# Forty prompt tokens instead of thirty-two by gathered value rows in a decoder layer's PEER stage

## The chip, the cores and the metric

The kernel runs on one core of a Trainium2 chip. The metric is the device time of one execution, in microseconds; lower is better. Three timed executions of the kernel before are given by their median. One further execution was taken with the hardware profiler; all rows of the trace are from that one.

## The reference, cut to what matters

One decoder layer is computed for 256 prompt tokens and 32 sample tokens (8 sequences of 4), D = 1024. After attention, convolution and projections comes PEER, a mixer with 16,384 experts. Each token picks 16 experts in each of 8 heads, so 128 per token.

```python
def chunk(xc):
    ...
    eid = jnp.take_along_axis(cand_id, top_j, axis=-1)
    gate = jax.nn.softmax(top_s, axis=-1)
    act = jax.nn.gelu(jnp.einsum('chkd,cd->chk', u_emb[eid], xc).astype(F32))
    return jnp.einsum('chk,chkd->cd', (gate * act).astype(v_emb.dtype), v_emb[eid])
```

`u_emb` and `v_emb` have 16,384 rows of 1024 numbers. Everything is float32.

## The kernel before

**Experts as tiles.** The 16,384 experts are 128 tiles of 128 experts; "expert c" below means tile c, 128x1024 numbers, 512 KB. The kernel does not gather `u_emb`: it computes every token's product with every expert. The *score stage* (from about 420 us) does this for tile 0 to 127: for all T = 288 tokens, a matmul with the stationary tile and the tokens as moving columns. To keep float32 accuracy in a faster matmul type, a tile is cut into a high and a low half; high x high, high x low and low x high are added, 24 matmuls of 288 columns per tile (lines 2300, 2301, 2307). The *output stage* (from about 864 us) does the weighted sum with the tiles of `v_emb`: for the TW = 224 prompt tokens that are done densely, the weights (gate x score, zero where a token did not pick the expert) are the moving columns. A tile costs eight matmuls `high` of 2 x 224 columns (value high with weights high and low, line 2358) and eight `lower` of 224 columns (line 2361).

**Tokens by gathered rows.** TG = 64 tokens, the 32 samples and the last 32 prompt tokens, don't pass through the output matmuls. Each has only 128 picks. 32 tokens x 128 picks are spread over the 128 partitions in 4 groups of 32 tokens, so 32 columns of picks for each set. For each column j POOL gathers a row of `v_emb` into each partition (`gather_row`, line 797, 512 KB) and the score of that pick from a copy in DRAM (`gather_score`, line 802, 4 bytes per partition). VectorE multiplies four columns of scores with their gates (`scale_picks`, line 1831) and adds row times weight to a sum (`add_row`, line 1840). At the end a matmul with the small matrix `fold` (four identities below one another) adds the partitions of each token: for the prompt set in `prompt_rows` (line 2396) between output experts 125 and 126, for the samples in `samples` (line 2388). The picks of the prompt set are computed in partitions 96 to 127 and brought into the pick tables by four moves, SBUF to SBUF, that SP issues after the stores of expert 31 (line 647, semaphore `moved`).

**Gates.** The dense weights need a gate matrix of 128 experts x 128 tiles per token. It is built beside score experts 32 to 87, in MIXED = 56 units of four tokens, one per expert: VectorE makes one-hots (lines 1768, 1769), TensorE multiplies them (`gate_tokens`, line 2336, two halves per unit, behind the high and the low matmuls of the expert), ScalarE copies (line 1158), VectorE adds (line 1778).

**Scores.** ScalarE applies gelu (line 1151) and SP stores the scores of experts 0 to 87 in DRAM (lines 637, 639; afterwards only the part of the 64 tokens, line 667), because the gates aren't ready. These 88 are read back in 22 reloads of four (`load_again`, line 661), into NACT = 5 buffers, three of which lie in the row buffers 2 to 4; VectorE multiplies them into the gates (`weights`, line 1805). Scores 88 to 127 are multiplied as they come (line 1810). Before the change reload j is issued at score expert 91 + 2j, the last three behind the tile loads of output experts 0 to 2. Products 72 to 87 are done beside output experts 0 to 15.

**What sets the order.** Each engine has a program written out by hand, with semaphores between them. Tiles come through a ring of R = 4 slots: `load_expert(c)` on SP (line 628) waits until both halves of tile c are cut, then loads tile c+4 into its slot. Then SP waits for the gelu of c and issues its stores, so whatever stands ahead of `load_expert` on SP delays tile and stores. ScalarE cuts the high halves (line 1090), at most two tiles ahead of TensorE, as `split` has two buffers; the gelu of expert c waits for the stores of expert c-2. The low halves are cut by POOL in the score stage (`cut_low`, line 784) and by VectorE in the output stage (`value_low`, line 1824). In the output stage ScalarE also makes the high weights (line 1192) and VectorE the low ones (`low`, line 1819); `high` waits for `w_lo`, `lower` for `lo_ready`. VectorE's order per output expert is `low`, `value_low`, for experts 0 to 15 one `weights`, and at the experts in ADD_AT an `add_row`, every fourth with `scale_picks` before it:

```python
FIRST_ADD, LAST_ADD = 6, NSUB - 5
ADD_AT = [FIRST_ADD + j * (LAST_ADD - FIRST_ADD) // (TG - 1) for j in range(TG)]
```

POOL's order after its last cut is: zero the sums, rows 0 and 1, wait for all score stores, scores 0 to 3, rows 2 to 4 (each as soon as its reload buffer is free), then for each further four columns: wait for `scale_picks` of the four before, four scores, four rows (each when the row five before it is added).

## Time and profile before

| what | value |
|---|---|
| timed executions | 1203.85 us median of 3 (1203.81 to 1205.47) |
| the profiled execution, its own time | 1208.57 us |
| its span, first to last instruction | 1206.8 us |
| TensorE busy | 1167.5 us |
| VectorE busy | 994.2 us |
| POOL busy | 709.6 us |
| ScalarE busy | 587.2 us |
| bytes moved by DMA | 278.73 MB, mean 231 GB/s |

TensorE is PE, VectorE DVE, ScalarE ACT, GpSimd POOL, SyncE SP; SPq is SP's queue of DMA issues. Busy time is the time in which an engine executes something; a matmul's record is longer than the step to the next one, since they overlap, so the pitch (start to start) is what counts. A releaser in brackets is what ended an idle time. The mean granted clock of a stretch is given as a share of 2.4 GHz, 1.00 being full.

### The profile page before, as it was taken

Reading aid. Unit: us, or ns where it says so; the run is one execution under the profiler, and the core shown is the slowest. Engines: PE = TensorE matmul, PEld = TensorE weight load, DVE = VectorE, ACT = ScalarE, POOL = GpSimd, SP = SyncE. Lnnn points to the kernel's source line nnn. Section 1 sums busy time; section 2 is a strip of 40 time slices with the busy share of each in tenths; the row PEclk is TensorE's granted clock in tenths of the full one; section 3 lists DMA queues with packets and bytes.
Section 4 is the critical chain, followed back from the end, with each engine's and each line's share of the span. In section 5 each row is a group of like instructions: output and inputs, shape, how many; then the busy total and the mean of one; then the engine's idle time right before and its main releaser. Section 6 shows DMA issues by size and latency. Waiting matters only on the chain. (4 is left out here: it accounts for less than half of the span.)

```text
span 1206.8 us, 27394 instructions
## 1 busy us (share of the span) xinstructions
PE 1167.5 (97%) x8823; PEld 1107.9 (92%) x8823; DVE 994.2 (82%) x2194; ACT 587.2 (49%) x1005; POOL 709.6 (59%) x377
## 2 busy tenths in 40 slices
PE   4999999989999999999999999999989999999998
PEld 3898888989989999999999999999989999999997
DVE  4899977866755999969999994998888888878886
ACT  2342445666444344445555554444455555555553
POOL 0475565612755667766666667777766556656531
PEclk9999999999999999999999999999999999999999
DMA  9796685424744356665555556777888899989883
GB/s 358 255 301 220 204 269 194 144 75 141 258 150 140 129 191 208 211 192 189 179 182 178 182 186 199 239 240 256 280 287 315 321 348 326 328 304 328 305 306 121
DMA packets 116800, 278.73 MB, mean 231 GB/s; under 512 B 33216, under 2 KB 54944, under 8 KB 116352
## 3 DMA queue, kind: packets, MB, share of 16 engines
q1 hardware_dynamic: 102928, 237.74, 58.6%
q0 software_dynamic: 12080, 36.51, 8.4%
q10 hardware_dynamic: 1728, 3.68, 0.9%
q8 instruction: 34, 0.56, 0.2%
q14 instruction: 30, 0.25, 0.1%
HBM read 259.41 MB, written 18.42 MB: 230 GB/s over the span
## 5 line engine op out<-in xcount | busy, mean ns | idle before, releaser
L784 POOL TENSOR_TENSOR split<-ring,split 128x1024 fp32r<-128x1024 f32 x128 | 310.2, 2423 | 132.0 <-ACT split L1090 132.0
L1090 ACT ACTIVATE split<-ring 128x1024 fp32r<-128x1024 f32 x256 | 271.6, 1061 | 147.9 <-PE ps L2358 72.1
L717 POOL TENSOR_TENSOR split<-ring,split 128x1024 fp32r<-128x1024 f32 x77 | 188.4, 2450 | 208.0 <-ACT split L901 207.9
L2300 PE MATMUL ps<-h2r,split 128*128 128x288 f32 x1024 | 278.5, 297 | 0.7 <-ACT big L1116 0.5
L2301 PE MATMUL ps<-h2r,split 128*128 128x288 f32 x1024 | 278.7, 296 | 0.0
L2358 PE MATMUL ps<-h2r,split 128*128 128x448 f32 x1016 | 230.9, 369 | 4.3 <-DVE h2r L1819 4.1
L2358 PEld LDWEIGHTS ps<-h2r,split 128*128 128x128 f32 x1016 | 182.3, 189 | 17.7 <-DVE h2r L1819 5.7
L2300 PEld LDWEIGHTS ps<-h2r,split 128*128 128x128 f32 x1024 | 193.0, 188 | 1.2 <-ACT big L1116 0.8
L2301 PEld LDWEIGHTS ps<-h2r,split 128*128 128x128 f32 x1024 | 192.5, 188 | 0.0
L1151 ACT ACTIVATE act<-ps 128x288 f32<-128x288 f32 x124 | 51.1, 412 | 218.3 <-PE ps L2307 218.2
L2307 PE MATMUL ps<-h2r,split 128*128 128x288 f32 x1024 | 156.6, 295 | 0.0
L1824 DVE TENSOR_TENSOR split<-ring,split 128x1024 fp32r<-128x1024 f32 x128 | 155.9, 1218 | 0.0
L2307 PEld LDWEIGHTS ps<-h2r,split 128*128 128x128 f32 x1024 | 141.6, 188 | 0.3 <-POOL split L784 0.3
L2361 PEld LDWEIGHTS ps<-h2r,split 128*128 128x128 f32 x1016 | 134.2, 192 | 3.3
L797 POOL DMA_INDIRECT big<-in_stream,pick_at x64 | 92.7, 1449 | 72.1 <-DVE big L1840 52.0
L2361 PE MATMUL ps<-h2r,split 128*128 128x224 f32 x1016 | 134.7, 274 | 0.0
L901 ACT ACTIVATE split<-ring 128x1024 fp32r<-128x1024 f32 x85 | 89.7, 1055 | 63.0 <-DMA ring<-in_stream 52.8
L802 POOL DMA_INDIRECT pick_act<-s_act_dram,pick_at x64 | 93.1, 1455 | 43.1 <-DVE pick_act L1831 20.7
L1769 DVE SCALAR_TENSOR_TENSOR hot<-ps,parts 128x256 fp32r<-128x256 f32 x224 | 107.1, 478 | 0.0
L1328 DVE SCALAR_TENSOR_TENSOR ps<-big,ps 128x256 f32<-128x256 f32 x232 | 95.7, 487 | 1.0
L1962 PE MATMUL ps<-h2r,split 128*128 128x288 f32 x552 | 90.9, 305 | 2.2 <-ACT split L901 1.2
L1819 DVE TENSOR_TENSOR h2r<-big,h2r 128x224 fp32r<-128x224 f32 x127 | 49.6, 391 | 47.6 <-ACT h2r L1192 35.8
(308 smaller groups left out, 1769.6 us busy)
## 6 DMA issues: line engine op xcount, KB each, us to landing
ring<-in_stream SPq DMA_DIRECT2D x371, 512.0 KB
big<-in_stream SPq DMA_DIRECT2D x20, 512.0 KB, 7.8
act_dram<-act SPq DMA_DIRECT2D x88, 112.0 KB, 1.7
big<-act_dram SPq DMA_DIRECT2D x17, 448.0 KB, 3.9
s_act_dram<-act SPq DMA_DIRECT2D x128, 32.0 KB, 1.5
parts<-act_dram SPq DMA_DIRECT2D x5, 448.0 KB
big<-in_cache_k SPq DMA_DIRECT2D x16, 128.0 KB, 2.5
big<-in_cache_v SPq DMA_DIRECT2D x16, 128.0 KB, 3.4
```

The source lines that it names most:

```text
L717: nc.gpsimd.tensor_tensor(split[:, n % 2, 1], ring[:, POS[CUT[n]] % R, :], split[:, n % 2, 0].bitcast(f32), ALU.subtract).then_inc(lin_lo, 1)
L784: nc.gpsimd.tensor_tensor(split[:, (n + ODD) % 2, 1], ring[:, slot_of(n), :], split[:, (n + ODD) % 2, 0].bitcast(f32), ALU.subtract).then_ ...
L802: pool.indirect_dma_start(pick_act[:, j:j + 1], None, s_act_dram, bass.IndirectOffsetOnAxis(ap=pick_at[:, 1, j:j + 1], axis=0))\
L1090: nc.scalar.activation(split[:, (n + ODD) % 2, 0], ring[:, slot_of(n), :], ACT.Copy).then_inc(hi_ready, 1)
L1328: ins = V.scalar_tensor_tensor(acc if j < CW - 1 else y[:, k, 0:TP], zp[:, k, j:j + TP], w, acc, ALU.mult, ALU.add)
L1769: return V.scalar_tensor_tensor(hot1[:, slot], iota_ps.unsqueeze(1).to_broadcast([P, 2, P]), parts[:, 0, col], parts[:, 2:4, col].to_broad ...
L1824: V.tensor_tensor(split[:, (n + ODD) % 2, 1], ring[:, slot_of(n), :], split[:, (n + ODD) % 2, 0].bitcast(f32), ALU.subtract).then_inc(lo_r ...
L2300: MM(out, u_hi[:, k], h_hi[:, k], start=(k == 0), stop=False)
L2301: last = MM(out, u_hi[:, k], h_lo[:, k], start=False, stop=False)
L2307: last = MM(out, u_lo[:, k], h_hi[:, k], start=False, stop=(k == KC - 1))
L2358: return MM(out, v[0][:, k], w, start=first, stop=last)
L2361: return MM(ps[k][:, 0:TW], v[1][:, k], w[:, 0], start=False, stop=False)
```

## The change

TC = 8 further prompt tokens go by gathered rows, so TG is 72 and TW 216. The eight lie with their 128 picks in 16 groups of 8 partitions, which makes 8 more columns (64 to 71), with tables, a third sum and a fold matrix of their own. MIXED is 54; experts 86 and 87 have no gate unit, 88 scores are still stored. SP issues 16 further moves. The 22 reloads are all issued in the score stage, at experts 89 to 93 and then every second one. POOL's first two row gathers stand before its cuts of experts 124 and 125. The memset of the sums is VectorE's. VectorE does `low` and `value_low` of output expert 0 before the product of score 127. The adds begin at output expert 8.

```diff
...
-TG = 2 * TS
+TC = 8
+TG = 2 * TS + TC
 TW = T - TG
 TURN = BEFORE - R
-AFTER = NSUB - MIXED - BEFORE
-assert BEFORE % R == 0 and MIXED % R == 0 and AFTER % R == 0 and NSUB % R == 0
-
-
-EARLY = (BEFORE + MIXED) // R
-NSTORED = BEFORE + MIXED
+NSTORED = BEFORE + -(-MIXED // R) * R
+AFTER = NSUB - NSTORED
+assert BEFORE % R == 0 and MIXED % 2 == 0 and AFTER % R == 0 and NSUB % R == 0
+
+
+EARLY = NSTORED // R
 LEFT_OVER = R
 AGAIN = (NSTORED // R - LEFT_OVER) * R
-assert NSTORED // R - LEFT_OVER + 1 <= 2 * (AFTER // R) - 1
+AGAIN_AT = [1, 2, 3, 4] + list(range(5, AFTER, 2))
+assert len(AGAIN_AT) >= NSTORED // R
...
             for part in range(4):
-                sp.dma_start(pick_at[part * TS:(part + 1) * TS, :, TS:TG], aside_u[P - TS:P, :, part * TS:(part + 1) * TS])\
+                sp.dma_start(pick_at[part * TS:(part + 1) * TS, :, TS:2 * TS],
+                             aside_u[P - TS:P, :, part * TS:(part + 1) * TS]).then_inc(moved, 16)
+            for part in range(P // TC):
+                sp.dma_start(pick_at2[part * TC:(part + 1) * TC], aside_u[P - TS - TC:P - TS, :, part * TC:(part + 1) * TC])\
                     .then_inc(moved, 16)
...
                     sp.wait_ge(gate_copied, 2 * MIXED)
-                    sp.wait_ge(moved, 16 * 5)
+                    sp.wait_ge(moved, 16 * (5 + P // TC))
                 else:
...
                     sp.dma_start(s_act_rows[g * R + n], act[:, n % 2, TW:T]).then_inc(act_stored[n % 2], 16)
-                    again = (g - EARLY) * 2 + n // 2 - 1
-                    if n % 2 and 0 <= again <= NSTORED // R - LEFT_OVER:
-                        load_again(again)
+                    if (g - EARLY) * R + n in AGAIN_AT[:NSTORED // R]:
+                        load_again(AGAIN_AT.index((g - EARLY) * R + n))
                 load_expert(NSUB + n, n)
-                if n < LEFT_OVER - 1:
-                    load_again(NSTORED // R - LEFT_OVER + 1 + n)
...
                 pool.indirect_dma_start(rows[:, j % NROW], None, value_rows,
-                                        bass.IndirectOffsetOnAxis(ap=pick_at[:, 0, j:j + 1], axis=0))\
+                                        bass.IndirectOffsetOnAxis(ap=mine_of(pick_at, pick_at2, slice(j, j + 1))[:, 0], axis=0))\
                     .then_inc(row_in[j % NROW], 16)
             def gather_score(j):
-                pool.indirect_dma_start(pick_act[:, j:j + 1], None, s_act_dram,
-                                        bass.IndirectOffsetOnAxis(ap=pick_at[:, 1, j:j + 1], axis=0))\
+                pool.indirect_dma_start(mine_of(pick_act, pick_act2, slice(j, j + 1)), None, s_act_dram,
+                                        bass.IndirectOffsetOnAxis(ap=mine_of(pick_at, pick_at2, slice(j, j + 1))[:, 1], axis=0))\
                     .then_inc(score_in, 16)
-            pool.wait_ge(gate_copied, 2 * MIXED)
-            nc.gpsimd.memset(s_sum, 0.0).then_inc(zeroed, 1)
-            pool.wait_ge(moved, 16 * 5)
-            for j in range(NROW - NACT + 2):
-                gather_row(j)
+            pool.wait_ge(moved, 16 * (5 + P // TC))
+            for n in range(R):
+                if n < NROW - NACT + 2:
+                    gather_row(n)
+                cut_low(NSUB - R + n, n, u_done, NSUB - R + (n - 1))
             for s in range(2):
...
             with eng.Fori(BEFORE // R, (BEFORE + MIXED) // R) as g:
-                turn(g, True)
+                turn(g, R)
+            if MIXED % R:
+                turn((BEFORE + MIXED) // R, MIXED % R)
             turn(NSTORED // R, False, stored=False, first=True)
...
             settle()
-            step(V.tensor_scalar(s_expert[:, 1], s_expert[:, 1], float(TS), None, ALU.add))
+            step(V.tensor_scalar(s_expert[:, 1], s_expert[:, 1], float(TS + TC), None, ALU.add))
+            for at, col in ((P - 2 * TS, TC - TS), (P - TS, TC)):
+                mine = theirs[at - part.start:at - part.start + TS, 1]
+                step(V.tensor_scalar(mine, mine, float(col), None, ALU.add))
+            step(V.tensor_reduce(fold2, ident[:, :].rearrange("p (g t) -> p t g", t=TC), AX.X, ALU.add))
             step(V.tensor_scalar(theirs[:, 0], theirs[:, 0], float((NLIN + NSUB) * P), None, ALU.add))
...
...
+            step(V.memset(s_sum, 0.0))
             done = 0
             for c in range(NSTORED, NSUB):
+                if c == NSUB - 1:
+                    low(0, 0, True)
+                    dve.wait_ge(lo_ready, NSUB)
+                    value_low(0, 0, u_done, NSUB - 1)
                 dve.wait_ge(gelued, c + 1)
                     done += 1
...
+            settle()
                 cols = slice(part * R, (part + 1) * R)
+                mine = mine_of(pick_act, pick_act2, cols)
                 dve.wait_ge(score_in, 16 * R * (part + 1))
-                V.tensor_tensor(pick_act[:, cols], pick_act[:, cols], pick_gate[:, cols], ALU.mult).then_inc(s_weighted, 1)
+                V.tensor_tensor(mine, mine, mine_of(pick_at, pick_at2, cols)[:, 2].bitcast(f32), ALU.mult).then_inc(s_weighted, 1)
...
                     dve.wait_ge(row_summed, j)
-                V.scalar_tensor_tensor(total, rows[:, slot], pick_act[:, j:j + 1], total, ALU.mult, ALU.add)\
+                V.scalar_tensor_tensor(total, rows[:, slot], mine_of(pick_act, pick_act2, slice(j, j + 1)), total, ALU.mult, ALU.add)\
                     .then_inc(row_summed, 1)
-            FIRST_ADD, LAST_ADD = 6, NSUB - 5
+            FIRST_ADD, LAST_ADD = 8, NSUB - 5
             ADD_AT = [FIRST_ADD + j * (LAST_ADD - FIRST_ADD) // (TG - 1) for j in range(TG)]
-            dve.wait_ge(zeroed, 8)
             j = 0
                     c = g * (2 * R) + i
-                    low(c, i % R, c == 0)
-                    value_low(c, i % R, *((u_done, NSUB) if c < 2 else (o_done, c - 1)))
+                    if c:
+                        low(c, i % R)
+                        value_low(c, i % R, *((u_done, NSUB) if c < 2 else (o_done, c - 1)))
                     if c < R * LEFT_OVER:
...
                     scores(g * R + (BEFORE + n), n, gates=lambda pair: gate_tokens(g * R + n, n, pair))
-            with pe.Fori((BEFORE + MIXED) // R, NSUB // R) as g:
+            for n in range(R if MIXED % R else 0):
+                mixed_at = MIXED // R * R + n
+                scores(BEFORE + mixed_at, n,
+                       gates=(lambda pair: gate_tokens(mixed_at, n, pair)) if mixed_at < MIXED else None)
+            with pe.Fori(NSTORED // R, NSUB // R) as g:
                 for n in range(R):
...
                 for k in range(KC):
-                    MM(ps[k][:, TW:TP], s_sum[:, 1, k * P:(k + 1) * P], fold[:, :], start=False, stop=False)
+                    MM(ps[k][:, TW:TW + TC], s_sum[:, 2, k * P:(k + 1) * P], fold2, start=False, stop=False)
+                    MM(ps[k][:, TW + TC:TP], s_sum[:, 1, k * P:(k + 1) * P], fold[:, :], start=False, stop=False)
             for n in range(R):

...
```

The functions `low` and `value_low` are unchanged and stand further up, so that the loop over the direct products can call them. `mine_of` picks the table of columns 0 to 63 or that of columns 64 to 71.

## Rows read from the trace of the kernel before

**Rows 1.** The page's part 1: busy us, share of the span, instructions.
```profile
PE 1167.5 (97%) x8823; PEld 1107.9 (92%) x8823; DVE 994.2 (82%) x2194; ACT 587.2 (49%) x1005; POOL 709.6 (59%) x377
```

**Rows 2.** The chain in order of time, output stage: start us, us, what.
```profile
1023.81 1.63 PE ps L2358 x8
1026.32 1.63 PE ps L2358 x8
```

**Rows 3.** TensorE's timeline, experts 34 and 35 with a gate unit: start us, us, line.
```profile
537.94 1.22 PE L2307 MATMUL ps<-h2r,split 128*128 128x288 f32 x8
541.63 1.22 PE L2307 MATMUL ps<-h2r,split 128*128 128x288 f32 x8
```

**Rows 4.** Stretches of the output stage: busy us (instructions) by engine, granted clock, DMA share, GB/s.
```profile
970.00:1010.00 40.00, 40.00 (x257) 38.15 (x256) 34.56 (x44) 22.03 (x32) 22.56 (x18) 1.00 0.97 347
1090.00:1130.00 40.00, 40.00 (x257) 38.10 (x256) 34.50 (x45) 21.91 (x32) 25.48 (x18) 1.00 0.89 310
```

**Rows 5.** The chain, fold of the prompt's gathered rows, 16 matmuls of 32 columns.
```profile
1192.08 1.71 PE ps L2396 x16
```

**Rows 6.** SP's timeline; lines 647 and 595, ns min/median/max; landing for line 661.
```profile
530.08 2.71 SPq L647 DMA_DIRECT2D pick_at<-big  x4
533.20 0.36 SPq L628 DMA_DIRECT2D ring<-in_stream  x1
...
L647 SPq DMA_DIRECT2D pick_at<-big x4: 598/606/767, 530.1 to 532.2; - x4
L595 SPq DMA_DIRECT2D big<-in_cache_v x16: 372/381/935, 46.8 to 175.9; - x16
...
DMA to landing us min/median/max: 3.7/3.9/4.2
```

**Rows 7.** Timelines of TensorE and VectorE in the gate stage; in brackets the idle time before.
```profile
542.68 0.40 PE L2336 MATMUL ps<-hot 128*128 128x256 f32 x2
...
530.81 0.35 DVE L1768 TENSOR_SCALAR hot<-ps,parts 128x128 fp32r<-128x128 f32 x1 [7.90 <-PE ps L2336]
```

**Rows 8.** TensorE's timeline at the junction of the stages, and the stretch around it.
```profile
858.36 1.23 PE L2307 MATMUL ps<-h2r,split 128*128 128x288 f32 x8
...
861.56 1.23 PE L2307 MATMUL ps<-h2r,split 128*128 128x288 f32 x8
864.71 2.73 PE L2358 MATMUL ps<-hot,split 128*128 128x448 f32 x8 [1.93 <-DVE hot L1819]
...
868.89 1.78 PE L2358 MATMUL ps<-h2r,split 128*128 128x448 f32 x8
...
862.00:869.00 7.00, 5.08 (x23) 4.60 (x23) 3.52 (x9) 2.69 (x4) 3.18 (x5) 0.76 0.90 325
```

**Rows 9.** Timelines of TensorE, VectorE and POOL around the stop at 902 us.
```profile
899.32 0.99 PE L2358 MATMUL ps<-h2r,split 128*128 128x448 f32 x4
...
905.15 2.34 PE L2358 MATMUL ps<-h2r,split 128*128 128x448 f32 x8 [3.15 <-DVE h2r L1819]
...
908.96 2.20 PE L2358 MATMUL ps<-h2r,split 128*128 128x448 f32 x8
...
903.25 0.16 DVE L1831 TENSOR_TENSOR pick_act<-pick_act,pick_at 128x4 f32<-128x4 f32 x1 [3.85 <-DMA pick_act<-s_act_dram,pick_at]
...
885.35 5.22 POOL L797 DMA_INDIRECT big<-in_stream,pick_at  x1 [8.05 <-DVE big L1805]
```

**Rows 10.** VectorE's instructions per output expert, page's part 5 and line 1840.
```profile
L1824 DVE TENSOR_TENSOR split<-ring,split 128x1024 fp32r<-128x1024 f32 x128 | 155.9, 1218 | 0.0
L1819 DVE TENSOR_TENSOR h2r<-big,h2r 128x224 fp32r<-128x224 f32 x127 | 49.6, 391 | 47.6 <-ACT h2r L1192 35.8
L1840 DVE SCALAR_TENSOR_TENSOR big<-big,pick_act x64: 1274/1280/1328, 882.1 to 1184.0; 128x1024 f32<-128x1024 f32 x64
```

**Rows 11.** POOL's cut and row gather, page's part 5.
```profile
L784 POOL TENSOR_TENSOR split<-ring,split 128x1024 fp32r<-128x1024 f32 x128 | 310.2, 2423 | 132.0 <-ACT split L1090 132.0
L797 POOL DMA_INDIRECT big<-in_stream,pick_at x64 | 92.7, 1449 | 72.1 <-DVE big L1840 52.0
```

More of the change, by code:

```diff
@@ L376, in build, with mine_of @@
         NROW = 5
+        s_sum = tail.take(3, D)
         rows = tail.take(NROW, D)
-        s_sum = tail.take(2, D)
         act_odd = tail.take(R, TW)
+        pick_at2 = tail.take(3, TC, dt=u32)
+        pick_act2 = tail.take(TC)
+        fold2 = tail.take(TC)
+        def mine_of(tile, tile2, cols):
+            return tile[..., cols] if cols.start < 2 * TS else tile2[..., cols.start - 2 * TS:cols.stop - 2 * TS]
         aside = rows[:, NROW - 1, 0:3 * P].rearrange("p (w n) -> p w n", n=P)
```

26 lines of the change are left out of this document (13 added, 13 removed).

## The prediction, made before the changed kernel was built or run

> **What bounds the kernel now.** I read the busy times, then the chain and timeline of TensorE, then the stretches, then the queues around each place that the diff touches. TensorE is busy for 97% of the span [rows 1], so time is won or lost only where it executes less or stands still. Busy isn't peak, so look at its pitch. In the output stage an expert is eight 448-column and eight 224-column matmuls; the first eight take 1.63 us and the whole repeats every 2.51 us [rows 2]. In the score stage an expert takes 3.20 us, with a gate unit in it 3.69 us [rows 3, 8]. Both stages run at TensorE's pitch, except where a queue is late. Two such places stand out: the junction of the stages [rows 8] and a stop at 902 us [rows 9]. The DMA queues (310 to 347 GB/s in the output stage, share 0.89 to 0.97) and VectorE (34.5 of 40 us) come next [rows 4].
>
> **The change, part by part** (minus is time saved).
>
> 1. *Narrower matmuls.* Each high matmul has 16 columns less, each low one 8. The widths give the price of a column: 1.63/8 = 203.75 ns at 448, (2.51-1.63)/8 = 110 ns at 224, so 0.42 ns per column, the full 2.4 GHz [rows 2]. An expert saves 8 x 24 x 0.4167 = 80 ns, 128 of them 10.2 us. The low matmul would go from 110 to 107 ns. The nearest row for a floor is the fold: 16 matmuls of 32 columns in 1.71 us, 107 ns each [rows 5]; it is just reached. If something near that floor holds the low one at 110 already, only the high ones gain: 6.8 us. I take **-10.2**, other end -6.8.
> The Trainium skill (TensorE: Matmul & The Clock Gate, LDWEIGHTS) puts a weight load at its columns over 1.2 GHz, 107 ns for 128. The fold's row agrees. By that rule the whole 10.2 us comes, and one column less on the low side would bring nothing.
>
> 2. *Two gate units fewer* (54 for 56): 3.69-3.20 = 0.49 us each [rows 3, 8]. **-1.0**.
>
> 3. *The junction.* The last eight score matmuls begin at 861.56, the first output matmul at 864.71, after 1.93 us of idling for VectorE's low weights; the first expert then takes 4.18 us instead of 2.51, at a mean granted clock of 0.76 between 862 and 869, so part of it ran at 1.2 GHz [rows 8]. The change does low(0) and value_low(0) ahead of the last direct product, which they don't need. Their inputs, ScalarE's high halves, are made during the last two score experts. Gone: 1.93 + 1.67 = **-3.6**; ends 0 and -3.6. Next late are the low weights of expert 1, behind the last product and two reload products: some 2 us after gelu, and expert 0 lasts 2.4.
>
> 4. *The stop at 902.* VectorE waited 3.85 us for the second four score gathers, TensorE then 3.15 us, and it restarted slowly: 5.83 and 3.81 us for two experts against 5.03, 4.6 us lost [rows 9]. POOL had come late to those gathers: it held the fifth row gather for VectorE's products of reload 19 and then needed 5.22 us for it, where 1.45 is the mean [rows 9, 11]. Now all reloads are issued within the score stage, the first adds move from expert 6 to 8 and the fifth from 13 to 14, and POOL's fifth row gather falls before the first add: about 3.5 us of slack more against 3.85 missing. Against that, experts 8 to 15 carry five adds beside the reload products: VectorE's work is 8 x (0.39+1.22+0.39) + 5 x 1.28 = 22 us by durations [rows 10], some 20 with the overlap of neighbours, in 19.5 us, and POOL finds few gaps. I take **-3.5**; ends -4.6 and 0.
>
> 5. *Fold of the eight tokens*: eight more calls, 16 matmuls of few columns: **+1.7** [rows 5].
>
> 6. *Sixteen more moves on SP.* SP finished the stores of expert 31, issued four moves from 530.08 (2.71 us, 0.68 each), and only then the tile load of expert 32's slot, at 533.20 [rows 6]. Now 20 moves stand there. A move of 8 partitions isn't in the trace. The nearest row is the four that are there, over 32 partitions: 0.60 us at least, 0.77 at most, and 0.05 between two; a copy over all 128 partitions on this queue takes 0.38 [rows 6]. I take 0.65, by the nearest: 16 x 0.65 = 10.4 us, so the load goes out at 543.6. It brings expert 36's tile. A 448 KB reload lands after 3.9 us [rows 6], 512 KB so after some 4.4; then ScalarE's cut, 1.1, and 0.1 for the signal: 549.2. TensorE was ready for expert 36 behind the gate matmuls of 542.68, at 542.95 [rows 7]. Behind the moves stand also expert 32's stores, for which the gelu of 34 waits, then its gate copies, VectorE's sum and one-hots, and TensorE's gates in expert 35; they too come to 549. So 6.2 us idle. The restarts after 1.9 and 3.15 us of idling cost 1.67 and 1.3 us [rows 8, 9]: 1.7 more. **+7.9**. Ends: at 0.42 each the moves take 6.7, 2.5 us idle, 4.2 in all; at 0.82 (0.77 and 0.05) 13.1, 9.0 idle, 10.7 in all. Nothing or a gain is excluded: the gelu of 34 can't pass the stores behind the moves.
>
> 7. *VectorE's picks* get two column shifts and one reduction, before the gates, where VectorE then stood idle for 7.90 us [rows 7]: hidden, **0**; without that cover 1 us. The memset leaves POOL for VectorE, where the wait for expert 88's gelu hides it. POOL's first two gathers go between its last four cuts: a cut takes 2.42 of 3.20 us, a gather 1.45 with 0.3 around it, so POOL is late by 0.5 to 1 us twice, about what its product was early. **+0.3**, ends 0 and 2. The reloads start two experts earlier, the first five in a row: 442 + 524 KB in 3.2 us is 302 GB/s, under the 347 that the queues carried [rows 4]: 0.
>
> 8. *More to carry in less time.* Each output expert brings a 524 KB tile, and a row gather now falls on each 1.62 experts (115 over 71) instead of each 1.86. That is 848 KB in 2.435 us, 348 GB/s, where it was 807 KB in 2.51 us, 321. One stretch ran at 347 with TensorE never idle, at a share of 0.97 [rows 4]: the load fits with almost nothing over. From 868.89 to the fold at 1192.08 are 323.2 us for 125 experts, 314.2 at their pitch: beside the stop, 4.4 us went in small delays [rows 5, 8]. VectorE's work per expert goes from 0.39+1.22+0.54 x 1.28 = 2.30 of 2.51 us to 2.40 of 2.435 by durations [rows 10], in truth some 0.2 us less in both. I put **+3.5**, nearly the 4.4 once more; ends 0 and 15.
> POOL's long gathers are those that meet VectorE without a gap [rows 9]. The Trainium skill (SBUF — State Buffer, Terms) has the two arbitrate for a port pair that is held for a whole instruction, the loser blocking. The trace agrees in that a gather that took 5.22 us ended during an add.
>
> Sum: -10.2-1.0-3.6-3.5+1.7+7.9+0.3+3.5 = **-4.9 us**. The profiled execution took 1208.57 us (span 1206.8 and 1.8 around it) and would take 1203.7. The three timed runs have a median of 1203.85, 4.7 lower; I take that difference over: **1199.0**.
>
> **Rivals.**
> - *Cheap moves.* At 0.42 us a move, term 6 is 4.2: 1195.3. For: a move has 768 bytes, a sixteenth of the four. Against: the four have little either and took longer than a 128 KB copy [rows 6]. Chance 0.2.
> - *The low matmuls don't shrink*, so the change doesn't do what it says: +3.4, 1202.4. For: 110 is near 107 ns. Against: 17 ns stand over the pure columns in both widths. Chance 0.1.
> - *The stop returns*, POOL starving behind a VectorE that has no gap in experts 8 to 15: term 4 is 0, and 1.5 us go at the third group: 1204.0. For: 22 us by durations in 19.5. Chance 0.1.
> - *The DMA queues become the bound, slower than before.* At 330 GB/s 848 KB take 2.57 us, 115 experts 295.5 us against 280.0: +15.5 in place of 3.5, 1211.0. It decides below 348 GB/s, eats the whole gain at 338 and is slower beyond the noise at 335. For: at 310 GB/s the share was 0.89 [rows 4]. Against: 347 for 40 us without a stop. Chance 0.15.
>
> **How the numbers follow.** The forecast has 0.45, with its own range 1194 to 1203. A measurement of this kernel tells 0.2% (2.4 us) from no change, so faster is below 1201.4 and slower above 1206.3. Faster: 0.38 of the forecast, 0.2 of the cheap moves, 0.06 of the low matmuls and the stop together: 0.64. Same: 0.06 of the forecast, 0.13 of these two, 0.03 of the DMA case: 0.22. Slower: 0.12 of the DMA case, 0.02 else: 0.14. Below 1191 (cheap moves, no stop and no new delay) lie 0.08, above 1207.5 some 0.11.
>
> **What would show it.** The output expert repeats every 2.435 us and the low matmul every 107 ns. TensorE has a gap of about 6 us near 543 us, a lower clock after it and SP's 20 moves before it. At the junction there is no gap. VectorE's wait for gathered scores in expert 14 is under 1 us. The DMA share is 0.95 or more from 900 to 1150. A gap near 543 of under 3 us makes the prediction too slow, a mean pitch over 2.46 us makes it too fast.

## The result, and the profile after

The changed kernel takes 1215.22 us (median of 5 executions, 1210.54 to 1220.68), the kernel before in the same session 1205.28 us: ratio 1.0089, 95% interval 1.0064 to 1.0113. It is slower by about 10 us, where 1199.0 was forecast and the range ended at 1207.5. The profiled execution took 1215.81 us (span 1214.0), that of before 1208.57.

The page's part 1 of the changed kernel, as in [rows 1]:
```profile
PE 1166.6 (96%) x8831; PEld 1111.5 (92%) x8831; DVE 951.2 (78%) x2188; ACT 588.8 (48%) x1001; POOL 724.3 (60%) x392
```
TensorE's busy time is the same to 1 us, though 128 experts have narrower matmuls; the span is 7.2 us longer.

**The moves.** SP's timeline, as in [rows 6], and the price of one move (ns min/median/max):
```profile
532.14 2.72 SPq L655 DMA_DIRECT2D pick_at<-big  x4
534.90 11.72 SPq L658 DMA_DIRECT2D big<-big  x16
547.04 0.35 SPq L636 DMA_DIRECT2D ring<-in_stream  x1
547.58 0.35 SPq L645 DMA_DIRECT2D act_dram<-act  x1
...
L658 SPq DMA_DIRECT2D big<-big x16: 685/686/788, 534.9 to 545.9; - x16
```
ScalarE's and TensorE's timelines there, as in [rows 7], then the stretches (engine columns as in [rows 4], then clock, DMA share, GB/s):
```profile
551.27 0.41 ACT L1159 ACTIVATE act<-ps 128x288 f32<-128x288 f32 x1 [11.69 <-DMA s_act_dram<-act]
...
543.70 1.21 PE L2328 MATMUL ps<-h2r,split 128*128 128x288 f32 x8
554.10 0.77 PE L2357 MATMUL ps<-hot 128*128 128x256 f32 x2 [9.19 <-DVE hot L1783]
...
558.38 1.22 PE L2328 MATMUL ps<-h2r,split 128*128 128x288 f32 x8
...
535.00:545.00 10.00, 9.91 (x76) 9.68 (x74) 6.74 (x20) 3.01 (x6) 4.79 (x2) 1.00 0.03 2
545.00:555.00 10.00, 0.90 (x4) 0.93 (x5) 2.82 (x9) 2.78 (x7) 1.59 (x1) 0.62 0.69 208
```
The tile load stands 14.90 us behind the first move, where it stood 3.12 behind [rows 6]. Call the eight matmuls with the low half of a tile its low phase; there is one for each expert. The interval between two low phases is 558.38 - 543.70 = 14.68 us instead of 3.69 [rows 3]: 11.0 us lost, 9.19 of idling and 1.8 of lower clock. For ten microseconds the DMA queues are nearly empty (share 0.03). What ended last is not the tile but the stores: issued at 547.6, they let the gelu go at 551.27.

**The junction** on TensorE's timeline, as in [rows 8]:
```profile
873.66 1.23 PE L2328 MATMUL ps<-h2r,split 128*128 128x288 f32 x8
...
877.25 1.81 PE L2383 MATMUL ps<-h2r,split 128*128 128x432 f32 x8
```
From the last score phase to expert 1 are 3.59 us, where they were 868.89 - 861.56 = 7.33: 3.7 us saved.

**The output stage**: a stretch that holds nearly the whole stage, with the columns of [rows 4].
```profile
880.00:1180.00 300.00, 294.88 (x1871) 283.79 (x1870) 261.09 (x335) 158.55 (x234) 199.61 (x142) 0.99 0.92 331
```
The same 300 us of the kernel before:
```profile
880.00:1180.00 300.00, 295.70 (x1856) 280.20 (x1855) 253.42 (x321) 159.77 (x233) 175.62 (x120) 0.99 0.89 315
```
The stop at 902 [rows 9] is gone, and there is one at 997 instead. ScalarE's, TensorE's and SP's timelines:
```profile
998.32 1.06 ACT L1098 ACTIVATE split<-ring 128x1024 fp32r<-128x1024 f32 x1 [5.32 <-DMA ring<-in_stream]
...
1000.12 2.14 PE L2383 MATMUL ps<-h2r,split 128*128 128x432 f32 x8 [3.49 <-DVE h2r L1825]
...
984.96 0.33 SPq L693 DMA_DIRECT2D big<-x_dram  x1
```
A tile was late, and SP had put the reload of x (1152 KB) ahead of it.

To compare whole stages I use one number below, **T**: from the start of the low phase of output expert 1 to that of expert 125. Delays are what T has over 124 undisturbed pitches. In the changed kernel:
```profile
878.90 1.04 PE L2386 MATMUL ps<-h2r,split 128*128 128x216 f32 x8
...
1196.57 1.05 PE L2386 MATMUL ps<-h2r,split 128*128 128x216 f32 x8
```
T = 317.7 us; the undisturbed pitch of 2.466 us would make it 124 x 2.466 = 305.8, so 12 us are delays. Before, T was 1191.03 - 870.51 = 320.5 at a pitch of 2.51 (311.2): 9.3 of delays. The pitch fell by 0.045 us, not by 0.075.

The two profiles differ by 7.2 us, and the parts add up to that within 0.1: 2.1 us are there when the score stage begins, 11.0 come with the moves, 1.0 go with the two gate units, 3.7 at the junction and 2.8 in T, and 1.7 come in the fold. The 2.1 lie within the scatter: in the 19 profiles of this document the score stage begins anywhere from 424.0 to 430.4 us.

### The profile page after: what moved, and what is told of

Its sections match the earlier page's. It is cut to its first block and busy times, and to the rows that moved or that the text cites. A ratio compares the mean times of both kernels' runs of the same rounds, so it can differ in the third digit from the quotient of the medians.

```text
span 1214.0 us, 27362 instructions
## 1 busy us (share of the span) xinstructions
PE 1166.6 (96%) x8831; PEld 1111.5 (92%) x8831; DVE 951.2 (78%) x2188; ACT 588.8 (48%) x1001; POOL 724.3 (60%) x392
## 5 line engine op out<-in xcount | busy, mean ns | idle before, releaser
L2383 PE MATMUL ps<-h2r,split 128*128 128x432 f32 x1016 | 226.1, 364 | 5.1 <-DVE h2r L1825 4.8
L2386 PE MATMUL ps<-h2r,split 128*128 128x216 f32 x1016 | 134.4, 274 | 0.0
L810 POOL DMA_INDIRECT pick_act<-s_act_dram,pick_at x64 | 88.8, 1387 | 38.8 <-issue 20.0
L1783 DVE SCALAR_TENSOR_TENSOR hot<-ps,parts 128x256 fp32r<-128x256 f32 x216 | 103.0, 477 | 0.0
L1841 DVE TENSOR_TENSOR big<-big,act 128x216 f32<-128x216 f32 x40 | 26.9, 673 | 78.9 <-ACT act L1159 78.9
```

The costliest lines, as they stand in the source:

```text
L1783: return V.scalar_tensor_tensor(hot1[:, slot], iota_ps.unsqueeze(1).to_broadcast([P, 2, P]), parts[:, 0, col], parts[:, 2:4, col].to_broad ...
L2383: return MM(out, v[0][:, k], w, start=first, stop=last)
L2386: return MM(ps[k][:, 0:TW], v[1][:, k], w[:, 0], start=False, stop=False)
```

## The experiments

Ratios are to the kernel before, on the same chip, with 95% intervals. T and "fold" (from the low phase of expert 125 to that of 126, with the prompt's fold in it) come from each kernel's one profile. e7 was executed once (1228.59 us) and isn't in the table; its T is 323.3.

| run | ratio | interval | T | fold |
|---|---|---|---|---|
| before | 1 | | 320.5 | 4.30 |
| after | 1.0089 | 1.0064, 1.0113 | 317.7 | 6.04 |
| e1_spread | 1.0024 | 1.0002, 1.0047 | 318.0 | 6.03 |
| e2_moves_only | 1.0109 | 1.0091, 1.0126 | 315.8 | 4.30 |
| e3_x_late | 1.0082 | 1.0063, 1.0100 | 321.8 | 6.03 |
| e4_x_late_before | 0.9996 | 0.9980, 1.0012 | 314.3 | 4.30 |
| e5_even | 1.0147 | 1.0104, 1.0189 | 329.5 | 7.21 |
| e6_half_rows | 1.0053 | 1.0032, 1.0074 | 317.5 | 8.37 |
| e8_junction_before | 1.0001 | 0.9973, 1.0030 | 316.3 | 4.30 |
| e9_early_before | 1.0009 | 0.9990, 1.0029 | 317.7 | 4.30 |
| e10_junction_early_before | 0.9970 | 0.9953, 0.9986 | 317.2 | 4.30 |
| e11_half_adds | 1.0108 | 1.0070, 1.0145 | 318.6 | 6.03 |
| e12_no_rows | 1.0038 | 1.0021, 1.0056 | 306.9 | 8.36 |
| e13_best_before | 0.9962 | 0.9934, 0.9990 | 316.8 | 4.29 |
| e14_best_after | 0.9996 | 0.9971, 1.0022 | 317.5 | 4.25 |
| e15_fewer_rows | 1.0068 | 1.0043, 1.0093 | 316.1 | 7.41 |
| e16_narrow_before | 0.9971 | 0.9936, 1.0007 | 315.7 | 4.26 |
| e17_no_rows_before | 1.0011 | 0.9992, 1.0031 | 312.7 | 4.30 |

(T of e14 is without the 1.8 us of the fold that it moves into that interval.)

**The moves: e1 and e2.**
```
 # e1: changed kernel; turns of experts 32 to 39 written out
-            for part in range(P // TC):
-                sp.dma_start(pick_at2[...], ...)        # 16 in a row
+                    sp.dma_start(s_act_rows[g * R + n], ...)
+                    for i in range(2):
+                        move(...)
...
 # e2: kernel before
+            for part in range(16):
+                sp.dma_start(extra_at[part * 8:(part + 1) * 8], aside_u[P - TS - 8:P - TS, :, part * 8:(part + 1) * 8])
```


> The changed kernel with its sixteen small moves two at a time behind the stores of experts 32 to 39, and the four wide ones where they stand. Theory (the moves cost SP some 0.7 us each, and TensorE waits because the next tile load and the stores stand behind them in one block): the interval of 14.68 us at 543 us becomes some 3.7 us plus at most the 3.1 us of the four wide moves that the kernel before already hides, and the time falls by about 11.0 us, from 1215.2 to about 1204, ratio to the kernel before about 1.000. Rival (SP is short of time in the gate stage too, with two stores and a load a unit): the two moves, 1.4 us, come late for the load in each of eight units of 3.69 us and cost up to 1 us each, so that only about 3 us come back: 1212.

> The kernel before with sixteen more moves of 8 partitions in the one place where its four moves stand; they copy to a place that nothing reads. Theory (the block of moves alone makes the stop): the interval at 541 us goes from 3.69 to about 14.7 us and the time rises by 11.0 us, ratio 1.0091. Rival (what was seen in the changed kernel needs its wider token set, or its other edits): a stop of 7.9 us as forecast, ratio 1.0066, or less. The second rival is that the later start of the tile stream lets the output stage win some of it back: then the stop is 11 us and the time rises by clearly less.

In e1 SP issues the same moves, two behind each pair of stores, and TensorE's low phases follow each other by 3.69 us (SP's and TensorE's timelines of e1):
```profile
533.21 1.56 SPq L658 DMA_DIRECT2D big<-big  x2
534.88 0.37 SPq L636 DMA_DIRECT2D ring<-in_stream  x1
...
533.05 1.22 PE L2339 MATMUL ps<-h2r,split 128*128 128x288 f32 x8
...
536.74 1.22 PE L2339 MATMUL ps<-h2r,split 128*128 128x288 f32 x8
```
e2 makes the stop of the changed kernel in the kernel before (its timelines):
```profile
534.91 11.72 SPq L651 DMA_DIRECT2D big<-big  x16
...
543.71 1.21 PE L2311 MATMUL ps<-h2r,split 128*128 128x288 f32 x8
...
558.01 1.22 PE L2311 MATMUL ps<-h2r,split 128*128 128x288 f32 x8
```
14.3 for 3.69 us, and 1.09% of the time, 13 us with 2 either way. The block alone makes the stop: the nine profiles with it have it at 10.6 to 11.3 us, and in e1 and e14, with the moves spread, it is gone. The rivals (SP too busy to carry two moves a turn, a smaller stop without the wider token set, the stage winning it back) fall. e1's ratio is 0.65% or 8 us below that of the changed kernel; with both intervals that is 4 to 12 us, so the stop's 11 may all have come back.

**The reload of x: e3 and e4.**
```
-            sp.wait_ge(w_lo, 24)
-            sp.dma_start(xe, x_dram).then_inc(x_loaded, 16)
-            with sp.Fori(11, NSUB // R - 1) as g:
-                v_turn(g)
+            with sp.Fori(11, NSUB // R - 1) as g:
+                v_turn(g)
+            sp.wait_ge(w_lo, 24)
+            sp.dma_start(xe, x_dram).then_inc(x_loaded, 16)
```


> The changed kernel with the reload of x (1152 KB) taken from the tile stream's middle to behind the last tile load. Theory (the reload runs at the moment when the tile stream has no slack, pushes the tiles behind it back and makes the stop at 995 to 1000 us): the stop of 5.3 us goes, the time falls by 4 to 5.3 us to about 1210.5, ratio about 1.0045, and nothing is lost at the end, since the reload lands within 3 to 4 us of its issue while four experts (9.9 us) are still to be computed. Rival (the output stage is short of DMA as a whole, so that the bytes cost their time wherever they stand): the stop only moves to another place or spreads over the small delays, and the time falls by less than 1.5 us.

> The kernel before with the same edit. Its trace shows a stop at 902 us, well ahead of where the reload is issued, and 4.4 us of small delays behind it. Theory (the reload hurts only where the stream is already late): no change beyond 0.1%, at most 1 us faster from small delays near 985 us. Rival (the bytes cost their time wherever the stream is busy): 2 us or more faster.

My theory fell. The delay at expert 48, the first tile behind the reload, is indeed the reload's: it is there with 1.2 us or more (at 47 or 48) in 7 of 15 profiles with the reload in the middle and in none of the 4 with it late. But the time didn't fall, neither in e3 nor in e4. e3 had another stop instead, at 1139 us. These are POOL's, SP's, ScalarE's and TensorE's timelines there, and what each DMA queue moved from 1128 to 1134 us (packets, MB, share of 16 engines):
```profile
1123.59 1.18 POOL L803 DMA_INDIRECT big<-in_stream,pick_at  x1 [0.30 <-issue]
...
1127.55 1.06 POOL L803 DMA_INDIRECT big<-in_stream,pick_at  x1 [0.30 <-issue]
...
1125.32 4.64 SPq L636 DMA_DIRECT2D ring<-in_stream  x2
...
1135.11 1.06 ACT L1096 ACTIVATE split<-ring 128x1024 fp32r<-128x1024 f32 x1 [3.15 <-PE ps L2381]
1138.08 0.38 ACT L1200 ACTIVATE h2r<-big 128x216 fp32r x1 [1.91 <-remote]
...
1138.93 2.30 PE L2381 MATMUL ps<-h2r,split 128*128 128x432 f32 x8 [3.13 <-issue]
...
q0 software_dynamic: 442, 1.57, 68.5%
q1 hardware_dynamic: 182, 0.68, 29.7%
```
Four rows of 512 KB, these two and two between them, were issued in 4 us. In the next 6 us the gathers' queue moved 1.57 MB and the tiles' queue 0.68 MB, 113 GB/s, where an expert's 524 KB in 2.466 us need 213. That isn't how the queues share the engines under equal load: SP issued no tile load between 1125.32 and 1129.94, so the tiles' queue had little to carry for part of that time. The Trainium skill (DMA: Bandwidth & Descriptors, SWDGE vs HWDGE vs iDMA) says that a DMA engine takes the queues in turn; no run here tests it. Nor is this stop a late tile alone: ScalarE had cut the tile by 1136.17 and then stood 1.91 us before its high weights (line 1200), which have no DMA to wait for in the program; the profile can't name what ended that wait, and VectorE and TensorE stood behind it.

**Order and bytes of the gathers: e5, e6, e12.**
```
 # e5: changed kernel, POOL; one score gather ahead of each row gather
-                    for j in range(part * R, (part + 1) * R):
-                        gather_score(j)
+                    gather_score(part * R)
+                for i in range(R):
+                    if part and i < R - 1: gather_score(part * R + i + 1)
+                    ... gather_row(part * R + i + 1)
 # e6
-            value_rows = a["stream"].rearrange("c p n -> (c p) n")
+            value_rows = a["stream"].rearrange("c p (h n) -> (c p h) n", h=2)
...
-                pool.indirect_dma_start(rows[:, j % NROW], ...)
+                pool.indirect_dma_start(rows[:, j % NROW, 0:D // 2], ...)
...
 # e12
                     pool.wait_ge(row_summed, j - NROW + 1)
-                    gather_row(j)
...
```


> The changed kernel with POOL's gathers in another order in the output stage: one score gather ahead of each row gather, where it had four score gathers and then up to four row gathers in one burst. Moves and reload stand as in the changed kernel. Theory (three or four row gathers of 512 KB in 4 to 5 us take so much of the DMA rate that the tile stream falls behind; the traces of the two kernels and of the one with the late reload each have their stop right behind such a burst, at 902, 997 and 1135 us): with the bursts gone the stop of 5.3 us and most of the 6.7 us of small delays go, TensorE loses under 4 us between the junction and the fold, and the time falls by about 8 us to about 1207, ratio about 1.002. Rival (the stage is short of DMA on the average, 36 MB of rows and 64 MB of tiles in 320 us are 313 GB/s): the delays spread out but stay, and the time falls by less than 2 us.

> The changed kernel with rows of 512 instead of 1024 elements gathered (from other places of the stream; the sum over the gathered rows is left wrong, the instructions and their order are as in the changed kernel, and VectorE clears 1504 more columns once). It takes 18 MB off the output stage's DMA. Theory (the delays of the output stage are DMA): no interval of TensorE in the output stage over 0.3 us late, and the time falls by 9 to 12 us to about 1205. Rival (the delays come from POOL's gather instructions holding VectorE off, as many of them as before): the delays stay and the time falls by less than 2 us.

> The changed kernel without the row gathers behind the first five (the adds stay and add stale rows; the 72 score gathers stay): 34 MB less in the output stage. Theory (bytes of rows make the tiles late): all delays of the output stage but the fold's are gone, ratio 1.0089 - 10/1205 = about 1.001. Rival (score gathers, with 128 packets of 4 bytes each, and VectorE's load make them): the delays stay above 5 us, ratio above 1.004.

e5 was 0.6% slower than the changed kernel, not faster. VectorE's timeline, and POOL's ahead of it:
```profile
1135.15 0.16 DVE L1855 TENSOR_TENSOR pick_act<-pick_act,pick_at 128x4 f32<-128x4 f32 x1 [6.54 <-DMA pick_act<-s_act_dram,pick_at]
...
1127.11 1.18 POOL L805 DMA_INDIRECT big<-in_stream,pick_at  x1 [0.30 <-issue]
1128.59 0.94 POOL L810 DMA_INDIRECT pick_act<-s_act_dram,pick_at  x1 [0.30 <-issue]
```
The last score gather of a group, 512 bytes in all, now stands in the queue behind a row of 512 KB: issued by 1129.5, it let VectorE go at 1135.15. My order made the wait that it should have removed. e6 gave back 0.36% for half of the bytes, with intervals that overlap: neither the 9 to 12 us of the theory nor the under 2 of the rival. Its output stage still had 12 us of delays, but by the profile few of them are late tiles: from 880 to 1180 us it puts down to tiles 2 waits of ScalarE, 2.3 us in all, and 44 waits, 66.2 us, in the changed kernel. Four of e6's five longest delays stand behind a wait of ScalarE before its high weights, such as this (its timeline):
```profile
981.90 1.06 ACT L1098 ACTIVATE split<-ring 128x1024 fp32r<-128x1024 f32 x1 [1.72 <-PE ps L2385]
985.64 0.38 ACT L1202 ACTIVATE h2r<-big 128x216 fp32r x1 [2.69 <-PE ps L2388]
```
The matmuls that these weights must wait for had ended at 981.8, so the releaser named isn't the real one, and what is stays open. e12, without the row gathers behind the first five, is clear in the stage: T comes down to 306.9 (low phases at 878.39 and 1185.32), 1.1 us over the plain pitch, and its 300 us read
```profile
880.00:1180.00 300.00, 299.60 (x1941) 290.85 (x1940) 270.81 (x347) 167.27 (x242) 102.17 (x75) 1.00 0.70 222
```
TensorE is idle for 0.4 of 300 us, with VectorE busier (270.8) and all score gathers in place. So the row gathers make the delays of the changed kernel's output stage, late tiles for the most part. That their bytes do it is not shown: e12 takes out POOL's instructions and the packets too, and e6, with half of the bytes and all of the rest, kept as much delay of another kind.

e12's time understates this. Its program ends 3.2 us later than its last store allows, because POOL's closing drain takes 8.41 us where it takes 4.32 in the changed kernel; without that its ratio would be about 1.0012, where 1.001 was expected. e17 below has the same.

**VectorE: e11.**
```
-                V.scalar_tensor_tensor(total, rows[:, slot], ..., total, ALU.mult, ALU.add)
+                cols = slice(0, 16 if j % 2 else D)
+                V.scalar_tensor_tensor(total[:, cols], rows[:, slot, cols], ..., total[:, cols], ALU.mult, ALU.add)
```


> The changed kernel with every second row added over 16 instead of 1024 columns (the rest of it is left out of the sum; all gathers stay, with all their bytes). It takes some 36 x 1.2 = 43 us of VectorE's work out of the output stage. Halving the rows' bytes instead gave only 3.6 us and left the delays. Theory (VectorE is the engine without slack there: 0.33 + 1.14 us an expert and 1.2 us in 72 of 128 of them are 2.15 of 2.466 us, so that it can't make up for a tile that comes late): small delays and stops shrink, the time falls by 5 us or more, to 1210 or below, ratio under 1.005. Rival (a late tile is late whatever VectorE does): less than 2 us.

Nothing came of 37 us less work (VectorE busy 914.0 us for 951.2): 1.0108. VectorE is not what keeps the stage from catching up.

**The junction and the early reloads: e8, e9, e10.**
```
 # e8: kernel before, VectorE
             for c in range(NSTORED, NSUB):
+                if c == NSUB - 1:
+                    low(0, 0, True)
+                    dve.wait_ge(lo_ready, NSUB)
+                    value_low(0, 0, u_done, NSUB - 1)
...
 # e9: kernel before with AGAIN_AT, the gathers between POOL's last cuts, the memset on VectorE, FIRST_ADD 8
 # e10: both
```


> The kernel before with only the order of the junction changed: VectorE makes the first value matrix's low parts ahead of its last direct product. Theory: the 3.74 us that the changed kernel saved there come whole, 1201, ratio 0.9969. Rival (the time is given back: the stream of tiles starts the output stage with less slack, and the stop behind it grows): ratio above 0.9985.

> The kernel before with the reloads and the first row gathers in the score stage, the adds from expert 8 and the sum's clearing on VectorE, and with the junction as it was. Theory (these edits clear the DMA queues and POOL ahead of the output stage): the stop near 902 us and the delay of the first output expert are gone, the time falls by 2 to 4 us, ratio about 0.9975. Rival (only the junction's own order counts): ratio 1.000 within 0.1%.

> Both: the early reloads and the junction's new order, in the kernel before. With the junction alone TensorE lost the 3.7 us again one expert later, where VectorE waited 3.63 us for a reload (448 KB) that had been issued only at 861.3 us. Theory (the two edits need each other): TensorE passes from the score stage to the second output expert without a wait, and the time is 3.5 to 7 us below the kernel before, about 1199.5, ratio 0.995. Rival (the sum of the two edits apart): the junction alone gave 1.0001, so this run is equal to the one with the early reloads alone.

Alone, neither pays. In e8 TensorE passes into expert 0 without a wait and then stands one expert later. TensorE's, SP's and VectorE's timelines of e8:
```profile
860.19 1.80 PE L2363 MATMUL ps<-hot,split 128*128 128x448 f32 x8
...
866.31 3.19 PE L2363 MATMUL ps<-h2r,split 128*128 128x448 f32 x8 [3.44 <-DVE h2r L1811]
...
861.27 0.37 SPq L661 DMA_DIRECT2D big<-act_dram  x1
...
865.46 0.39 DVE L1805 TENSOR_TENSOR big<-big 128x224 f32<-128x224 f32 x1 [3.63 <-DMA big<-act_dram]
```
VectorE needs a reload that SP issued only at 861.27. With the reloads early (e10's TensorE) the wait is gone:
```profile
860.88 1.23 PE L2312 MATMUL ps<-h2r,split 128*128 128x288 f32 x8
...
864.58 1.85 PE L2363 MATMUL ps<-h2r,split 128*128 128x448 f32 x8
```
3.70 us to expert 1, and 0.9970: the two edits need each other.

**Widths: e7.**
```
+                HW = 192 if inner and n == 3 else TW
+                LW = (TW, 192, 128, TW)[n] if inner else TW
```


> The changed kernel with other widths in the output stage: of every four experts the first as it is, the second with low matmuls of 192 instead of 216 columns, the third of 128, the fourth with high matmuls of 2 times 192 instead of 2 times 216 (the columns beyond are left out of the product). Theory (a low matmul has a floor of 110 ns, which columns below 224 don't move): the eight low ones take 0.88 us at 216, 192 and 128 columns, the first three pitches are equal, 2.466 us, and the fourth is shorter by 8 x 48 x 0.42 ns = 0.16 us, 2.31 us. Rival (columns count, and 216 against 224 was too small a step to see): second pitch 2.39 us, third 2.17 us.

TensorE's timeline of e7:
```profile
949.78 1.04 PE L2390 MATMUL ps<-h2r,split 128*128 128x216 f32 x8
950.66 1.74 PE L2387 MATMUL ps<-h2r,split 128*128 128x432 f32 x8
952.24 1.03 PE L2390 MATMUL ps<-h2r,split 128*128 128x192 f32 x8
953.11 1.75 PE L2387 MATMUL ps<-h2r,split 128*128 128x432 f32 x8
954.70 1.00 PE L2390 MATMUL ps<-h2r,split 128*128 128x128 f32 x8
955.54 1.64 PE L2387 MATMUL ps<-h2r,split 128*128 128x384 f32 x8
957.02 1.04 PE L2390 MATMUL ps<-h2r,split 128*128 128x216 f32 x8
```
From start to start eight low matmuls take 0.88, 0.87 and 0.84 us at 216, 192 and 128 columns: 110, 109 and 105 ns each. So 88 columns less bring 5 ns, not the 37 that 0.42 ns a column would give: that is the floor. The eight high ones take 1.58 us at 432 and 1.48 at 384 columns, 0.10 less where 0.16 were expected.

**What is left, and what pays: e13 to e17.**
```
 # e13: e10 and the late reload of x. e14: e1, the late reload, and
-                if n == 1: prompt_rows()        # 32 matmuls
+                if n < 2: prompt_rows(n)        # 16 and 16
 # e15: changed kernel
+                    if j % 9 != 8:
                         gather_row(j)
...
 # e16: kernel before
+                W = TW if first or last else TW - 8        # in high() and lower()
 # e17: kernel before with e12's edit
```


> The kernel before with the junction, the early reloads and the late reload of x: 32 prompt tokens gathered as before, no small moves. Theory (the parts of the change that pay, without those that cost; of the late reload of x 0.5 us at most by the two runs with it): 1201, ratio 0.9965. Rival (the late reload helps where the stream is tight: with the junction's edits alone one stop of 1.3 us is left at expert 48, the first tile behind that reload): 1199.5, ratio 0.995.

> The changed kernel with the small moves spread, the reload of x late, and the prompt fold in two parts of 16 matmuls behind two experts. Three theories add: the spread moves bring the ratio to 1.0024, the late reload takes the delay at expert 48 (2.4 us in the run with the spread moves, where it stood alone), and the split fold keeps the granted clock at 1.00 (in four of the eight profiles with 32 narrow matmuls in a row it fell to 0.50 there, which made the interval 1.2 to 2.3 us longer, so 1 us on the average): ratio 1.000. Rival (the rows' bytes make their delay wherever they land): 1.0024 or above.

> The changed kernel without the gather of every ninth row (64 gathered as before the change, 72 added, eight of them stale; 4 MB less in the output stage, evenly). Theory (the eight rows' bytes are what raised the output stage's delays from some 7 to some 12 us): the time falls by 3 to 5 us, ratio near 1.005. Rival (the shorter pitch of 2.466 us asks for the same tiles in less time, and that raised them): less than 1.5 us, ratio 1.0075 or above.

> The kernel before with its output matmuls 8 columns narrower (216 for 224, the last eight tokens' product left out in experts 1 to 126; 64 rows gathered, all else as before). Theory (the high matmuls give 0.0475 us an expert, the low ones nothing): pitch 2.466 us, 5.9 us less, ratio 0.995. Rival (with DMA near its limit the shorter pitch is given back in late tiles): under 3 us of it stays, ratio above 0.9975.

> The kernel before without the row gathers behind the first five (the adds stay and add stale rows; the 64 score gathers stay). In the changed kernel the same edit took the output stage's first-to-last interval (low phase of expert 1 to that of expert 125) from 317.7 to 306.9 us, against 305.5 at the plain pitch. Theory (both kernels' output stage lasts as long as the DMA queues need, about 317 us with 64 rows, and the plain pitch is hidden beneath): here it comes down to 311.2 us and a little, 312, and the time falls by 4 to 6 us, ratio 0.9955. Rival (before the change the stage ran at TensorE's pitch and its delays had other causes): over 315 us, ratio above 0.9985.

e16 has the widths of the changed kernel with the bytes of the one before. Its pitch is 2.447 us, and not the 2.466 of the changed kernel at the same columns; why is open. By that its experts 1 to 126 need 8.3 us less than before. Its T, 315.7, is only 1.2 us under the mean of the seven profiles with the old pitch and all bytes (316.9: before, e2, e4, e8, e9, e10, e13), where the pitch gives 8.2. Its time says -0.29%, 3.5 us, with an interval from 7.7 us less to 0.8 more. So by T most of the gain was lost with no byte added; by the time it may be anything from nearly none to all, and how much is open. e15 took 0.2% off the changed kernel, with overlapping intervals. The five profiles with the new pitch and 72 rows (after, e1, e3, e11, e14) have a mean T of 318.7, 1.8 us more than those seven with 2.4 either way by their scatter, although the matmuls need 5.5 less: none of the pitch's gain, or at most a small part, reached the stage's length.

e17 went against my theory: on its chip, where the kernel before took only 1201.35 us, leaving out the row gathers made nothing faster, though T was 312.7. Part of this is the end of its program. The closing instructions of e17 (POOL's drain, ns; SP's branch behind its last store, start):
```profile
L207 POOLq DRAIN  x1: 7757/7757/7757, 1192.5 to 1192.5; - x1
...
L207 SPq COMPARE_BRANCH  x1: 38/38/38, 1197.5 to 1197.5; - x1
```
The drain ends at 1200.2, 2.7 us after SP is through; in the kernel before it takes 3.02 us and ends 2 us ahead of SP. Without the 2.6 us that this costs, e17's ratio would be about 0.999, still above the 0.9955 of the theory. So the row gathers cost the kernel before at most 3 or 4 us on that chip, where they cost the changed kernel some 11 us of T, by e12, on another. No run has both kernels without their rows on one chip, so chip and kernel aren't told apart.

e14 brings the changed kernel level with the one before, and no further. e13 and e10 beat both: 0.9962 and 0.9970.

The fold showed something that neither text had foreseen. A stretch of 2 us in the fold, of the changed kernel:
```profile
1199.00:1201.00 2.00, 2.00 (x20) 2.00 (x19) 0.71 (x1) 0.00 (x0) 0.00 (x0) 1.00 0.00 0
```
and of e12:
```profile
1190.00:1192.00 2.00, 2.00 (x8) 1.91 (x9) 0.00 (x0) 0.00 (x0) 0.00 (x0) 0.50 0.00 0
```
TensorE is busy throughout in both, with matmuls of 8 and 32 columns, and in e12 the clock falls to 1.2 GHz. It fell in one profile each of four of the eight timed kernels with 32 such matmuls in a row, and in e7 (fold 7.2 to 8.4 us instead of 6.0), in none of those with 16, and not in e14, which splits them. In e12 the matmuls behind that interval, too, took 0.9 us longer. Why it fell in some and not in others is open.

## Why the prediction was wrong, step by step

- *The last step, "I take that difference over"*: wrong by about 3.5 us. The profiled execution of before stood above its median and had the stop at 902 in it. I subtracted the stop as a saving (step 4) and then subtracted the difference as well. The four later profiles with the old order of reloads and all gathers (e2, e4, e8, e16) show nothing more than the pitch at experts 14 and 15, and e17 1.0 us. It was an accident of that execution, not a cost of the kernel.
- *Step 1, narrower matmuls*, -10.2: the high ones came near the forecast (198.4 ns for 197.1), the low ones stayed at 110 ns. I had the floor as a rival at 0.1, and took the 107 ns of the Trainium skill (TensorE: Matmul & The Clock Gate, LDWEIGHTS) as leave to go 3 ns lower; the trace doesn't show that step. Measured -5.7 at the pitch (128 x 0.045 us); e7 shows the floor. Here row and rule were both near and the rival deserved half.
- *Step 6, the moves*, +7.9: measured 11.0 in the profile. The move cost 0.73 us from start to start, not 0.65, which is 1.3 us. The larger part of the rest is the sentence "they too come to 549": the stores went out behind the tile load and took 3.7 us until the gelu, and behind it stood the gate copies and VectorE's one-hots, so that TensorE began 22.0 us behind the first move instead of 19.1. The rival of cheap moves, at 0.2, has nothing for it.
- *Step 3, the junction*, -3.6: right (-3.7), but by e8 and e10 only together with the early reloads, which the text took as costing 0 and saving nothing.
- *Step 2*, -1.0: right (the score stage from expert 36 on takes 315.3 us for 316.3). *Step 5*, +1.7: right (the fold's interval grew by 1.74 us). Missed is the clock: 1.2 to 2.3 us more in that interval in some executions.
- *Step 8, more to carry*, +3.5: too small. With the gain of the pitch counted under step 1, the output stage lost 5.5 + 1.8 = 7.3 us, with 2.4 either way, to delays. The rival "the DMA queues become the bound" is the nearest to what e12 shows, with 1211.0 the nearest of all my numbers, though e6 speaks against its bytes as the whole cause. Its decision point, a rate below 348 GB/s, was the right question: the stage ran at 331. "347 for 40 us without a stop" misled me: a stretch that is carried at a share of 0.97 doesn't say that bursts will be. I also left the reload of x out of the bytes; e3 and e4 show that its place costs nothing to be seen in the time.
- *Step 7*: nothing seen against it.
- The signs named beforehand pointed the right way: the pitch was 2.466 us (over 2.46, so too fast a forecast), the DMA share 0.92 and not 0.95, and TensorE's gap at the moves 9.2 us and not 6.

From the median of before, 1205.3: -5.7 -1.0 -3.7 +1.7 +11.0 +7.3 and about 1 for the clock in the fold are +10.6, against +10 measured. Since the terms come from the same profiles, this shows that nothing large is missing and no more. The size of the +7.3 is the loosest: it rests on profiles, one for each kernel, which scatter by 6 us with the same bytes.

Open: what in the row gathers delays the stage, their bytes, packets or instructions; what ScalarE waits for before its high weights in e3 and e6; why the same bytes cost so differently from execution to execution, and from chip to chip (medians of before from 1201.35 to 1206.84); and whether gathers issued a group ahead, in even steps, would keep the tiles on time, which wasn't tried.

## What to carry to other kernels

Never correct a sum for a profiled execution's distance from the median and count its stops as savings too: first see whether a second profile has the stop. A block of small DMA issues holds back what stands behind it on its queue, however few its bytes: here 16 of 768 bytes cost 11 us. With two behind each turn, as in e1, no stop was left. In a stage whose DMA share is already 0.89, don't count the gain of narrower matmuls as time: here none of it, or little, was seen in the stage's length, so adding bytes and shortening the compute must be priced together. And when an experiment leaves work out, look at the end of its program too: e12 and e17 lost 2.6 to 3.2 us there.

## What was not expected of the hardware

- A move of 8 partitions and 768 bytes cost SP 0.69 us (0.73 with the gap), as much as one of 32 partitions (0.68 apiece), where a load of 512 KB over all partitions took 0.35.
- A matmul of 128 to 224 columns took 105 to 110 ns in this loop; at 384 and 432 columns it took 185 and 198. The same 432 columns took 195.6 ns in e16.
- 32 matmuls of 8 and 32 columns in a row, with TensorE busy at 2.00 of 2.00 us, were followed by a granted clock of 0.50 in five of nine profiles.
- Without the row gathers POOL's closing drain took 7.8 and 8.4 us instead of 3.0 and 4.3, and it was what ended last.
- ScalarE stood 1.9 to 2.7 us before its high weights in e3 and e6 with nothing in the profile that it waited for.
